# Attention block: the softmax moved to the front of VectorE's period, and two units of the output product's second half begun under the last head

## The chip, the core and the metric

One core of a Trainium2 chip. The metric is device time of one execution in microseconds (us), the median over runs. Engine names in the profile: PE is TensorE's matmul, PEld its weight load, DVE is VectorE, ACT is ScalarE, POOL is GpSimd, SP the engine that issues the DMAs.

## What is computed

Two transformer blocks run one after the other, each of two layers, on 256 tokens (the first one on 272, with 16 tokens put in front) and a model width of 1024, in float32. The first block is FFN, mixer, FFN in each layer. The mixer of its second layer is the one that the change touches, a differential attention with eight heads, cut here to what matters:

```python
q, k, v = jnp.split(h @ w_qkv, 3, axis=-1)      # 8 heads, q and k in two parts of 64, v of 128
q, k = partial_rope(q), partial_rope(k)
...
p = softmax(where(mask, q @ k.T * scale, NEG_INF))
a = p[:, :, 0] - lam * p[:, :, 1]
o = rms_norm(a @ v, subln_g, SUBLN_EPS) * (1.0 - lambda_init)
m = o.reshape(bsz, seq_len, d) @ w_o
h = h + rms_norm(m, g)
```

## The kernel before

**Products.** Activations stand transposed: a chunk is 128 features in the partitions by the tokens in the free dimension, and the width of 1024 is eight chunks. A product with a weight matrix is cut into units. A unit is 128 output features: eight chunks of weights, each 128 by 128. Both operands are split into a high and a low part (`x_hi`, `x_lo`; `w_hi`, `w_lo`), and `product` issues three matmuls for a chunk: high by high, high by low, low by high. So a unit has 24 matmuls. Four units are a quad, and their weights have four slots in SBUF (`raw`, `w_hi`, `w_lo`).

**The path of a unit's weights.** SP loads `raw` of a slot as soon as VectorE has split the slot's previous content (semaphore `w_lo_ready`). ScalarE writes `w_hi` (`split_hi`, line 581) when `raw` has landed and TensorE has finished the slot's previous unit (`unit_done`). VectorE then writes `w_lo` = `raw` - `w_hi` (`split_lo`, line 1046). TensorE waits for `w_lo_ready`. Whole units are split at once, 1024 columns. The stages of the kernel take the slots in turn. Here they are `ain` (the projection to q, k and v, 24 units), `aout` (the output product `w_o`, 8 units in two quads), and then `gu3` (the next FFN).

**The attention.** Every engine has its own list of work, written out by hand in a loop over periods `p`. In period `p` TensorE computes the three units of head `p` (q, k, v) and, between them, the later steps of the heads `p-1` and `p-2`:

```python
for p in range(2, HEADS):
    ain_unit(3 * p)
    swapped(p - 1)
    ain_unit(3 * p + 1)
    attn_t(p - 2)
    ain_unit(3 * p + 2)
    head_sum(p - 2)
    scores(p - 1)
    square_sum(p - 2)
```

`swapped` is a helper product for the rope (lines 1960, 1962). `scores` computes the two score matrices into banks 4 and 6 of PSUM and transposes v (lines 1970 to 1980). `attn_t` transposes the finished probabilities (lines 1987 to 1991); it waits for VectorE's last softmax instruction, `aB` on line 1364. `head_sum` multiplies them with v (lines 1997 to 1999), after ScalarE's copies on lines 808 to 810. `square_sum` sums the squares for the head's norm (line 2003).

ScalarE's part of a head: it takes q and k out of PSUM (lines 799, 804), computes the exponentials (`exps`, four instructions and four reads of the accumulator, line 832), copies the transposed probabilities (`attn_t`), squares the head's output (`out_square`, line 814), computes its norm (lines 603, 605), and a period later writes the high part of the output (`upper_out`, line 838). Between these stand the splits of weights.

VectorE's period is `att_split(u)` (the `w_lo` of one unit), `lower_out(p-3)` (line 1376, the low part of a head's output), `softmax(p-2)` (six instructions, lines 1356 to 1364, that begin when the exponentials of head `p-2` are there), `rope(p-1)` (six instructions, lines 1328 to 1336), `att_split(u+1)`, `value(p)`, `att_split(u+2)`, `maxima(p-1)`, `full_out(p-2)` (line 1371). Each engine does its list strictly in order.

**The output product.** Its first quad needs the heads as its chunks: chunk `k` is head `k`'s output. TensorE takes those chunks in `aout_part` calls as they become ready, mixed with the last heads' steps: before the last head's `attn_t` it computes chunks 0 to 6 of the units 0 to 3, and chunk 7 when the last head is finished. The second quad (`aout_last`) begins after that. Its weights are split in `out1` of ScalarE and `evac_out1` of VectorE: for output `o`, ScalarE waits for the unit, squares it (line 735), takes it out of PSUM with a gain (line 736), and then splits the next unit for the slot. GpSimd adds the squares up (`add0` to `add6`, line 1693). TensorE puts the sum of the seven into the norm's bank (`res_most`, line 1861) before chunk 5 of the last unit, and the eighth square after it (`res_last`, line 1866). From this ScalarE computes the norm (lines 603, 605), VectorE adds it to `h` (lines 1092, 1098), and the next stage's first quad begins (lines 1801 to 1809). `out1_bank` names the PSUM bank of each unit; the norm's sum is always in bank 4.

`vec.phase`, `act.phase` and `pe.phase` at line 344 and after only declare the order in which each engine counts up its semaphore.

## Time and profile before

| | |
|---|---|
| median of 3 runs | 1411.38 us (1411.13 to 1411.57) |
| the profiled execution's own time | 1414.27 us |
| its span in the profile | 1412.5 us |
| mean granted clock of TensorE | 0.982 |
| TensorE busy | 1341.3 us, 95% |
| VectorE busy | 920.4 us, 65% |
| ScalarE busy | 807.2 us, 57% |
| read from HBM | 237.76 MB, 169 GB/s |

The span is the part of the execution that the profile shows, from the first instruction to the last. Busy time of the matmuls is modelled (they overlap), so how far apart two of them start says more than how long each is. "Idle before" in a row, written [1.03 <-DVE arena L1364], is the time for which the engine stood still before that instruction, and what released it. The granted clock is 1.00 at 2.4 GHz and 0.50 at 1.2 GHz; a stretch that has both shows a value between. The attention with its output product lies from about 755 to 902 us of the span.

### The profile page before, as it was taken

How to read it: one execution, taken by the hardware profiler on the slowest of the kernel's cores; microseconds unless marked ns; L12 is line 12 of the kernel's file. 1: busy time of each engine (PE TensorE's matmuls, PEld its weight loads, DVE VectorE, ACT ScalarE, POOL GpSimd, SP SyncE). 2: the span in 40 equal slices, each digit the busy share in tenths (PEclk: the TensorE clock that was granted, in tenths of full speed). 3: DMA queues.
4: the chain of work that ended last, by engine and by line, in shares of the span. 5: the costliest groups of instructions: out<-in, count | busy, mean ns of one | idle time of the engine just before them, and what ended most of it. 6: DMA issues, size and time to landing. Idle time of an engine off the chain costs nothing.

```text
span 1412.5 us, 27540 instructions
## 1 busy us (share of the span) xinstructions
PE 1341.3 (95%) x10214; PEld 1292.3 (91%) x10214; DVE 920.4 (65%) x1522; ACT 807.2 (57%) x1567; POOL 82.1 (6%) x81
## 2 busy tenths in 40 slices
PE   6999999998999999999998998899999899989997
PEld 6999999998999999999998886899999899977786
DVE  6777537856777537777437665677764575666774
ACT  6666534447666536666535553776664444457662
POOL 2000001012000001000001000400000000010000
PEclk9999999999999999999999999999999899999999
DMA  5767653663666653767643331466665153444440
GB/s 199 250 228 239 219 192 107 188 189 114 229 223 245 218 163 98 235 229 251 209 125 120 105 105 46 134 224 223 227 250 166 56 179 120 137 129 148 124 121 31
DMA packets 63313, 239.98 MB, mean 170 GB/s; under 512 B 7024, under 2 KB 8448, under 8 KB 63104
## 3 DMA queue, kind: packets, MB, share of 16 engines
q1 hardware_dynamic: 63168, 238.84, 51.4%
q8 instruction: 56, 0.92, 0.3%
q14 instruction: 25, 0.20, 0.0%
q0 software_dynamic: 64, 0.02, 0.0%
HBM read 237.76 MB, written 1.05 MB: 169 GB/s over the span
## 4 chain that ended last, share of the span: by engine, by line
PE 73%; DVE 12%; ACT 9%; issue 4%; DMA 1%; DVEq 0%; ACTq 0%; SPq 0%
PE bank L1736 19%; PE bank L1738 19%; PE bank L1737 19%; DVE w_lo L1046 5%; ACT w_hi L581 3%; PE bank L1743 3%; ACT ada_raw L657 2%; PE bank L1808 1%; PE bank L1801 1%; PE bank L1809 1%; PE bank L1744 1%; DMA ada_raw<-ada_w 1%; PE bank L2103 1%; DVE ada_raw L1134 1%; ACT ln_t L603 1%
## 5 line engine op out<-in xcount | busy, mean ns | idle before, releaser
L1046 DVE TENSOR_TENSOR w_lo<-raw,w_hi 128x1024 fp32r<-128x1024 f32 (+1 forms) x376 | 493.5, 1316 | 338.8 <-ACT w_hi L581 338.5
L1736 PE MATMUL bank<-x_hl,w_hi 128*128 128x272 f32 (+1 forms) x1776 | 516.3, 291 | 14.6 <-DVE w_lo L1046 14.4
L1738 PE MATMUL bank<-x_hl,w_lo 128*128 128x272 f32 (+1 forms) x1776 | 510.9, 288 | 0.0
L1737 PE MATMUL bank<-x_hl,w_hi 128*128 128x272 f32 (+1 forms) x1776 | 509.1, 287 | 0.0
L581 ACT ACTIVATE w_hi<-raw 128x1024 fp32r<-128x1024 f32 (+1 forms) x376 | 413.8, 1106 | 130.4 <-PE bank L1738 110.8
L1736 PEld LDWEIGHTS bank<-x_hl,w_hi 128*128 128x128 f32 x1776 | 335.6, 189 | 17.7 <-ACT arena L617 8.6
L1737 PEld LDWEIGHTS bank<-x_hl,w_hi 128*128 128x128 f32 x1776 | 338.2, 190 | 0.6
L1738 PEld LDWEIGHTS bank<-x_hl,w_lo 128*128 128x128 f32 x1776 | 335.1, 189 | 0.0
L1736 PE MATMUL bank<-a_hi,w_hi 128*128 128x272 f32 (+1 forms) x960 | 278.8, 290 | 14.5 <-DVE w_lo L1046 3.9
L1738 PE MATMUL bank<-a_hi,w_lo 128*128 128x272 f32 (+1 forms) x960 | 275.3, 287 | 0.0
L1737 PE MATMUL bank<-a_lo,w_hi 128*128 128x272 f32 (+1 forms) x960 | 274.7, 286 | 0.0
L1736 PEld LDWEIGHTS bank<-a_hi,w_hi 128*128 128x128 f32 x960 | 182.5, 190 | 18.1 <-DVE w_lo L1046 7.6
L1737 PEld LDWEIGHTS bank<-a_lo,w_hi 128*128 128x128 f32 x960 | 182.9, 191 | 0.3
L1738 PEld LDWEIGHTS bank<-a_hi,w_lo 128*128 128x128 f32 x960 | 182.3, 190 | 0.0
L657 ACT ACTIVATE ada_raw<-ada_raw,cond 128x128 f32<-128x128 f32 x384 | 117.6, 389 | 0.9 <-DMA ada_raw<-ada_w 0.7
L673 ACT ACTIVATE a_hi<-arena 128x272 f32 (+3 forms) x88 | 37.7, 429 | 125.5 <-DVE arena L1152 125.1
L1743 PE MATMUL bank<-x_hl,w_hi 128*128 128x512 f32 x256 | 93.5, 405 | 4.4 <-DVE x_hl L1084 2.8
L1744 PE MATMUL bank<-x_hl,w_lo 128*128 128x256 f32 x256 | 72.2, 282 | 0.0
L1743 PEld LDWEIGHTS bank<-x_hl,w_hi 128*128 128x128 f32 x256 | 48.7, 190 | 16.2 <-issue 5.0
L1680 POOL TENSOR_TENSOR sq_sum<-sq_sum,sq 128x272 f32<-128x272 f32 (+1 forms) x28 | 21.4, 765 | 701.8 <-ACT sq L706 701.8
L706 ACT ACTIVATE sq<-bank 128x272 f32<-128x272 f32 (+1 forms) x32 | 12.6, 395 | 85.9 <-PE bank L1738 85.9
L1808 PE MATMUL bank<-x_hl,w_hi 128*128 128x272 f32 (+1 forms) x144 | 43.9, 326 | 10.6 <-ACT x_hl L613 8.3
(273 smaller groups left out, 1427.7 us busy)
## 6 DMA issues: line engine op xcount, KB each, us to landing
raw<-w SPq DMA_DIRECT2D x312, 512.0 KB, 4.5
raw<-w SPq DMA_DIRECT2D x64, 704.0 KB, 4.8
ada_raw<-ada_w SPq DMA_DIRECT2D x48, 512.0 KB, 3.6
h<-x_in SPq DMA_DIRECT2D x1, 1088.0 KB, 5.1
work<-bands SPq DMA_DIRECT2D x1, 544.0 KB, 7.0
cst<-consts SPq DMA_DIRECT2D x1, 528.0 KB, 4.6
out<-h SPq DMA_DIRECT2D x1, 512.0 KB, 3.0
out<-h SPq DMA_DIRECT2D x4, 128.0 KB, 2.3
```

The source lines that it names most:

```text
L581: sc.activation(w_hi[:, s, 0:n], raw[:, s, 0:n], ACT.Copy).then_inc(w_hi_ready, 1)
L603: sc.activation(ln_t[:, 0:n], src, ACT.Ln, bias=eps[:, :], scale=scale).then_inc(act.step(phase, "ln"), 1)
L657: last = sc.activation(ada_raw[:, c, :], ada_raw[:, c, :], ACT.Copy, scale=cond[:, c:c + 1])
L673: sc.activation(a_hi[:, bass.ds(2 * i + p, 1), 0:n].rearrange("p a t -> p (a t)"), u_t[:, p, 0:n], ACT.Copy).then_inc(act.step(phase, f"hi ...
L1046: ve.tensor_tensor(w_lo[:, s, 0:n], raw[:, s, 0:n], w_hi[:, s, 0:n].bitcast(F32), ALU.subtract).then_inc(w_lo_ready, 1)
L1680: gp.tensor_tensor(sq_sum[:, 0:n], sq_sum[:, 0:n], sq[:, p, 0:n], ALU.add).then_inc(pool.step(phase, f"add{p}"), 1)
L1736: te.matmul(dst, w_hi[:, s, a:a + P], rhs_hi, start=first, stop=False)
L1737: te.matmul(dst, w_hi[:, s, a:a + P], rhs_lo, start=False, stop=False)
L1738: return te.matmul(dst, w_lo[:, s, a:a + P], rhs_hi, start=False, stop=last)
L1743: te.matmul(dst.rearrange("p (a t) -> p a t", a=2), w_hi[:, s, a:a + P], both, start=first, stop=False)
L1744: return te.matmul(dst[:, 0:SEQ], w_lo[:, s, a:a + P], both[:, 0, :], start=False, stop=last)
L1808: te.matmul(dsts[s][:, 0:n], w_hi[:, s, k * P:(k + 1) * P], x_hi[:, k, 0:n], start=k == 0, stop=False)
```

## The change

In every period VectorE does `softmax(p-2)` first, ahead of `att_split(u)` and `lower_out(p-3)`; before, it came after both.

Of the output product's second quad, chunks 0 to 5 of the units 0, 1 and 2 are computed ahead of the quad's own place: units 0 and 1 around the last head's `square_sum`, ahead of chunk 7 of the first quad, and unit 2 behind unit 1 of the second quad. For that the weights of these three units are split in two pieces. The piece for chunks 0 to 5 (768 columns) is split in period 9 by `early_hi` and `early_lo`, once TensorE has done chunk 5 of the slot's unit of the first quad; the piece for chunks 6 and 7 (256 columns, from `6 * P`) at the old place. In TensorE's list chunk 5 of the units 0 and 1 now comes before unit 3, and chunk 6 of the four units comes behind the last head's transposes instead of ahead of them. The units of the second quad are in other banks (4, 6, 3, 7 for 3, 6, 7, 0), so the wait for the free bank is now `f0` of the second quad, ahead of `res_most`.

```diff
--- before.py
+++ after.py
@@ -344,10 +344,12 @@
 
         vec.phase("att", ["ib", "cb", "cr", "sr"])
         for p in PERIODS:
+            if head(p - 2):
+                vec.phase(f"soft{p - 2}", ["r", "l", "bA", "aA", "bB", "aB"])
             if head(p - 3):
                 vec.phase(f"lo{p - 3}", ["lo"])
-            if head(p - 2):
-                vec.phase(f"soft{p - 2}", ["r", "l", "bA", "aA", "bB", "aB"])
+            if p == HEADS + 1:
+                vec.phase("early", ["lo0", "lo1", "lo2"])
             if head(p - 1):
                 vec.phase(f"rope{p - 1}", ["qc", "kc", "qx", "kx", "qs", "ks"])
             if head(p):
@@ -363,10 +365,14 @@
                 act.phase("preas", ["ln", "r"])
             if head(p - 3):
                 act.phase(f"hi{p - 3}", ["hi"])
+            if p == HEADS + 1:
+                act.phase("early", ["hi0", "hi1"])
             if head(p) and p:
                 act.phase(f"k{p}", ["k"])
             if head(p - 2):
                 act.phase(f"at{p - 2}", ["atm", "at1", "at2"])
+                if p == HEADS + 1:
+                    act.phase("early2", ["hi2"])
                 act.phase(f"osq{p - 2}", ["osq"])
             if head(p - 1):
                 act.phase(f"vn{p - 1}", ["vn", "vm"])
@@ -386,6 +392,8 @@
                 pe.phase(f"s{p - 1}", ["s0", "s1", "vt"])
             if head(p - 2):
                 pe.phase(f"oss{p - 2}", ["oss"])
+            if p == HEADS:
+                pe.phase("early", ["u0", "u1", "u2"])
         declare_out1("aout", "resa")
         declare_enter("pre3")
         declare_ffn(3)
@@ -497,7 +505,9 @@
 
             if stage == "eout":
                 return bank[((6, 7, 0, 1), (2, 3, 5, 6))[i][s]]
-            if stage in ("aout", "oout"):
+            if stage == "aout":
+                return bank[((0, 1, 2, 5), (4, 6, 3, 7))[i][s]]
+            if stage == "oout":
                 return bank[((0, 1, 2, 5), (3, 6, 7, 0))[i][s]]
             return bank[s]
 
@@ -571,14 +581,14 @@
 
         @block.scalar
         def _(sc):
-            def split_hi(stage, i, s):
+            def split_hi(stage, i, s, a=0):
 
                 n = W11 if wide(stage) else W8
                 q = FIRST_QUAD[stage] + i
                 sc.wait_ge(raw_in[s], 16 * q + 16)
                 if not (isinstance(i, int) and q == 0):
                     sc.wait_ge(unit_done, SLOTS * q - SLOTS + s + 1)
-                sc.activation(w_hi[:, s, 0:n], raw[:, s, 0:n], ACT.Copy).then_inc(w_hi_ready, 1)
+                sc.activation(w_hi[:, s, a:n], raw[:, s, a:n], ACT.Copy).then_inc(w_hi_ready, 1)
 
             def split_next(stage, i, s):
 
@@ -734,7 +744,9 @@
                             sc.wait_ge(pool.sem, pool.at(stage, f"add{o - 2}"))
                         sc.activation(sq[:, o % 2, 0:n], out1_bank(stage, i, s)[:, 0:n], ACT.Square).then_inc(act.step(stage, f"sq{s}"), 1)
                         sc.activation(f[:, o, 0:n], out1_bank(stage, i, s)[:, 0:n], ACT.Copy, scale=gain(res, o)).then_inc(act.step(stage, f"f{s}"), 1)
-                        if o < 7:
+                        if stage == "aout" and o < 3:
+                            split_hi(stage, 1, s, 6 * P)
+                        elif o < 7:
                             split_next(stage, i, s)
                 res_norm(res)
 
@@ -837,6 +849,12 @@
                 sc.wait_ge(vec.sem, vec.at(f"full{h}", "full"))
                 sc.activation(a_hi[:, h, META:T], head_out, ACT.Copy).then_inc(act.step(f"hi{h}", "hi"), 1)
 
+            def early_hi(phase, s):
+
+                sc.wait_ge(raw_in[s], 16 * (FIRST_QUAD["aout"] + 1) + 16)
+                sc.wait_ge(pe.sem, pe.at("early", f"u{s}"))
+                sc.activation(w_hi[:, s, 0:6 * P], raw[:, s, 0:6 * P], ACT.Copy).then_inc(act.step(phase, f"hi{s}"), 1)
+
             for p in PERIODS:
                 u = 3 * p
                 if head(p) and p:
@@ -846,11 +864,16 @@
                     token_norm("prea", bank[4])
                 if head(p - 3):
                     upper_out(p - 3)
+                if p == HEADS + 1:
+                    early_hi("early", 0)
+                    early_hi("early", 1)
                 if head(p) and p:
                     raw_k(p)
                     att_split(u + 1)
                 if head(p - 2):
                     attn_t(p - 2)
+                if p == HEADS + 1:
+                    early_hi("early2", 2)
                 if head(p):
                     att_split(u + 2)
                 if head(p - 2):
@@ -1038,12 +1061,12 @@
 
         @block.vector
         def _(ve):
-            def split_lo(stage, i, s):
+            def split_lo(stage, i, s, a=0):
 
                 n = W11 if wide(stage) else W8
                 q = FIRST_QUAD[stage] + i
                 ve.wait_ge(w_hi_ready, SLOTS * q + s + 1)
-                ve.tensor_tensor(w_lo[:, s, 0:n], raw[:, s, 0:n], w_hi[:, s, 0:n].bitcast(F32), ALU.subtract
+                ve.tensor_tensor(w_lo[:, s, a:n], raw[:, s, a:n], w_hi[:, s, a:n].bitcast(F32), ALU.subtract
                                  ).then_inc(w_lo_ready, 1)
 
             def split_next(stage, i, s):
@@ -1214,7 +1237,10 @@
 
             def evac_out1(stage):
                 for o in range(7):
-                    split_next(stage, o // SLOTS, o % SLOTS)
+                    if stage == "aout" and o < 3:
+                        split_lo(stage, 1, o, 6 * P)
+                    else:
+                        split_next(stage, o // SLOTS, o % SLOTS)
 
 
             ve.wait_ge(params_in_, 16)
@@ -1376,14 +1402,25 @@
                 ve.tensor_tensor(a_lo[:, h, META:T], head_out, a_hi[:, h, META:T].bitcast(F32), ALU.subtract
                                  ).then_inc(vec.step(f"lo{h}", "lo"), 1)
 
+            EARLY = 6 * P
+
+            def early_lo(s):
+
+                ve.wait_ge(act.sem, act.at("early2" if s == 2 else "early", f"hi{s}"))
+                ve.tensor_tensor(w_lo[:, s, 0:EARLY], raw[:, s, 0:EARLY], w_hi[:, s, 0:EARLY].bitcast(F32), ALU.subtract
+                                 ).then_inc(vec.step("early", f"lo{s}"), 1)
+
             for p in PERIODS:
                 u = 3 * p
+                if head(p - 2):
+                    softmax(p - 2)
                 if head(p):
                     att_split(u)
                 if head(p - 3):
                     lower_out(p - 3)
-                if head(p - 2):
-                    softmax(p - 2)
+                if p == HEADS + 1:
+                    for s in range(3):
+                        early_lo(s)
                 if head(p - 1):
                     rope(p - 1)
                 if head(p):
@@ -2002,7 +2039,14 @@
                 te.wait_ge(act.sem, act.at(f"osq{h}", "osq"))
                 te.matmul(bank[7][:, 0:SEQ], ones[:, :], sq[:, 0, 0:SEQ], start=True, stop=True).then_inc(pe.step(f"oss{h}", "oss"), 1)
 
-            def aout_part(units, heads):
+            def early_part(s, heads):
+
+                te.wait_ge(vec.sem, vec.at("early", f"lo{s}"))
+                te.wait_ge(act.sem, act.at(f"e{HEADS - 1}", "eB1"))
+                for k in heads:
+                    product(out1_bank("aout", 1, s)[:, 0:SEQ], s, k, a_hi[:, k, META:T], a_lo[:, k, META:T], k == 0, False)
+
+            def aout_part(units, heads, step=None):
 
                 for s in units:
                     te.wait_ge(w_lo_ready, SLOTS * FIRST_QUAD["aout"] + s + 1)
@@ -2013,6 +2057,8 @@
                                        k == 0, k == DC - 1)
                         if k == DC - 1:
                             last.then_inc(unit_done, 1)
+                        if step:
+                            last.then_inc(pe.step(step, f"u{s}"), 1)
 
             te.wait_ge(tables_in, 80)
             swapped(0)
@@ -2041,21 +2087,26 @@
             scores(last)
             square_sum(last - 1)
             te.wait_ge(act.sem, act.at(f"vn{last}", "vm"))
+            aout_part((0, 1), range(5, 6), "early")
             aout_part((3,), range(0, 6))
-            aout_part((0, 1, 2), range(5, 6))
+            aout_part((2,), range(5, 6), "early")
+            attn_t(last)
             aout_part((0, 1, 2, 3), range(6, 7))
-            attn_t(last)
             head_sum(last)
+            early_part(0, range(0, 3))
             square_sum(last)
+            early_part(0, range(3, 6))
+            early_part(1, range(0, 6))
             aout_part((0, 1, 2, 3), range(7, 8))
 
             def aout_last():
                 for s in range(SLOTS):
+                    if s == 2:
+                        early_part(2, range(0, 6))
                     te.wait_ge(w_lo_ready, SLOTS * FIRST_QUAD["aout"] + SLOTS + s + 1)
-                    if s == 3:
-                        te.wait_ge(act.sem, act.at("aout", "f0", 0))
-                    for k in range(DC):
+                    for k in range(6 if s < 3 else 0, DC):
                         if s == 3 and k == 5:
+                            te.wait_ge(act.sem, act.at("aout", "f0", 1))
                             res_most("resa", pool.at("aout", "add6"))
                         last = product(out1_bank("aout", 1, s)[:, 0:SEQ], s, k, a_hi[:, k, META:T], a_lo[:, k, META:T],
                                        k == 0, k == DC - 1)
```

## Rows read from the trace of the kernel before

**Rows 1.** The page: busy us (share of the span) xinstructions by engine.
```profile
PE 1341.3 (95%) x10214; PEld 1292.3 (91%) x10214; DVE 920.4 (65%) x1522; ACT 807.2 (57%) x1567; POOL 82.1 (6%) x81
```

**Rows 2.** Waits from 765 to 857 us: engine, tile, line <- releaser: us, times, longest.
```profile
PEld bank L1987 <- DVE arena L1364: 8.1, 6, 1.8
...
PE bank L1987 <- DVE arena L1364: 6.8, 6, 1.6
```

**Rows 3.** Timeline of one period: start us, us, engine, line, operation, tiles.
```profile
784.36 0.21 ACT L832 ACTIVATION_READ_ACCUMULATOR arena<-bank,small 128x1 f32 x1
...
786.37 1.23 DVE L1046 TENSOR_TENSOR w_lo<-raw,w_hi 128x1024 fp32r<-128x1024 f32 x1 [2.94 <-ACT w_hi L581]
...
787.84 0.17 DVE L1356 RECIPROCAL small<-small 128x4 f32<-128x4 f32 x1
...
788.56 0.29 PE L1738 MATMUL bank<-x_hl,w_lo 128*128 128x272 f32 x1
...
789.32 0.50 DVE L1364 SCALAR_TENSOR_TENSOR arena<-arena,small 128x272 f32<-128x272 f32 x1
...
789.88 0.28 PE L1987 MATMUL bank<-cst,arena 128*16 128x128 f32 x1 [1.03 <-DVE arena L1364]
```

**Rows 4.** Timeline: what comes next in that period.
```profile
791.17 0.25 ACT L810 ACTIVATE arena<-bank 128x128 f32<-128x128 f32 x1
...
799.54 0.21 ACT L832 ACTIVATION_READ_ACCUMULATOR arena<-bank,small 128x1 f32 x1
```

**Rows 5.** Timeline of the last head: its softmax, copies and sums.
```profile
869.98 0.39 PE L1736 MATMUL bank<-a_hi,w_hi 128*128 128x256 f32 x1 [0.19 <-ACT vn L820]
...
872.26 0.21 ACT L832 ACTIVATION_READ_ACCUMULATOR arena<-bank,small 128x1 f32 x1
...
873.15 0.17 DVE L1356 RECIPROCAL small<-small 128x4 f32<-128x4 f32 x1
...
875.19 0.28 PE L1987 MATMUL bank<-cst,arena 128*16 128x128 f32 x1 [0.15 <-DVE arena L1364]
...
876.78 0.69 PE L1997 MATMUL bank<-arena,vn 16*128 16x256 f32 x2 [0.88 <-ACT arena L810]
...
878.80 1.12 PE L2003 MATMUL bank<-sq,ones 128*128 128x256 f32 x2 [0.47 <-ACT sq L814]
...
881.94 0.43 DVE L1376 TENSOR_TENSOR a_lo<-arena,a_hi 128x256 fp32r<-128x256 f32 x1 [0.48 <-ACT a_hi L838]
882.51 0.55 PE L1736 MATMUL bank<-a_hi,w_hi 128*128 128x256 f32 x1 [2.59 <-DVE a_lo L1376]
```

**Rows 6.** Timeline of the output product's second half.
```profile
883.52 0.38 ACT L735 ACTIVATE sq<-bank 128x256 f32<-128x256 f32 x1 [1.62 <-PE bank L1738]
...
884.05 0.73 POOL L1693 TENSOR_TENSOR sq_sum<-sq_sum,sq 128x256 f32<-128x256 f32 x1 [127.89 <-ACT sq L735]
884.16 1.06 ACT L581 ACTIVATE w_hi<-raw 128x1024 fp32r<-128x1024 f32 x1
...
886.53 0.39 PE L1736 MATMUL bank<-a_hi,w_hi 128*128 128x256 f32 x1 [1.12 <-DVE w_lo L1046]
...
887.22 1.53 POOL L1693 TENSOR_TENSOR sq_sum<-sq_sum,sq 128x256 f32<-128x256 f32 x1 [0.15 <-ACT sq L735]
...
896.88 0.59 PE L1861 MATMUL bank<-sq_sum,ones 128*128 128x256 f32 x2
...
898.57 0.38 ACT L735 ACTIVATE sq<-bank 128x256 f32<-128x256 f32 x1 [1.56 <-PE bank L1738]
```

**Rows 7.** Stretches: us, then each engine's busy us and count, granted clock, DMA.
```profile
878.00:885.00 7.00, 3.94 (x17) 3.06 (x15) 0.91 (x2) 3.17 (x7) 0.73 (x1) 0.57 0.01 2
888.00:898.00 10.00, 10.00 (x85) 9.95 (x85) 6.84 (x6) 6.95 (x13) 5.49 (x5) 1.00 0.89 306
902.00:905.40 3.40, 2.98 (x14) 2.71 (x15) 3.25 (x7) 1.97 (x6) 0.00 (x0) 0.62 0.03 8
858.00:865.00 7.00, 5.90 (x45) 5.31 (x45) 4.83 (x15) 3.28 (x14) 0.00 (x0) 1.00 0.16 61
```

## The prediction

> **What bounds the kernel now.** I read the page's busy times first: TensorE is busy for 1341.3 of 1412.5 us, the others for at most 65% [rows 1]. So time can only come from TensorE's gaps or from stretches at its lower clock. Next the list of waits over the attention's periods: TensorE waits there for one thing that counts, the last softmax instruction of VectorE, six times, 6.8 us in all by the matmuls and 8.1 us by the weight loads, which start ahead of them; the longest is 1.6 or 1.8 us [rows 2]. The timeline of one period shows why [rows 3]. The exponentials are finished at 784.57. VectorE stands idle until ScalarE has written the next unit's high part, splits that unit (1.23 us from 786.37), does the low part of a head's output, and begins the softmax only at 787.84. It ends at 789.82, and TensorE, whose unit's last matmul started at 788.56, starts the transposes at 789.88.
>
> Last I read the end of the attention in order of time. TensorE stands idle for 0.88 us before the last head's sum and for 2.59 us before chunk 7 [rows 5], and for 1.12 us before the second quad [rows 6]. From 878 to 885 us the granted clock is 0.57, mostly the lower level of 1.2 GHz, after the stretch with these waits [rows 7].
>
> **The periods.** Moving the softmax adds no instruction. It then follows the exponentials at once, 784.6, and its length is 789.82 - 787.84 = 1.98 us, so it ends at 786.6. TensorE arrives at 788.56 + 0.13 = 788.69 (two neighbouring matmuls of 256 columns start 10.00 / 85 = 0.118 us apart [rows 7], those of 272 columns by that 0.125). The wait goes entirely, with 1.9 us to spare. What it costs is 789.88 - 788.69 = 1.19 us in each of five periods and 1.62 + 0.16 = 1.78 in the first (0.16 is the part of the previous matmul that the next one overlaps): 5 x 1.19 + 1.78 = **7.7 us**. The ends are 6.8 and 8.1 us, the two sums of the wait.
>
> What is late next? The `w_lo` that now stands behind the softmax is that of a unit four units ahead in TensorE's list; it comes about 0.3 us later and is wanted a period later, and SP's next load for that slot moves with it. The rope begins when softmax, split and low part are through (1.98 + 1.23 + 0.42 = 3.6 us after 784.6, so 788.2; it was 789.8), so it moves forward by more than TensorE does. ScalarE's copies of the transposed probabilities ended at 791.42 [rows 4], 1.54 us behind the start of the transposes. TensorE's unit behind them takes 3.2 us. With the copies now behind a split of 1.05 us they end at 2.4 us, still inside it. The next exponentials end at 799.75 [rows 4], 9.87 us after the transposes; a period is 799.54 - 784.36 = 15.2 us and the new one 14.0, so the next softmax (1.98) ends 2 us before it is wanted. Nothing takes the wait's place.
>
> **The last head.** All times from here are in the old trace's own; the 7.7 us come off them all. In period 8 and in the last, the low part (0.43 us, of which the next instruction covers some 0.1) goes behind the softmax. At the last head the exponentials end at 872.47 and the softmax began at 873.15 [rows 5]; it can begin 0.64 us earlier. In period 8 the rope then follows 0.64 - 0.35 = 0.3 us earlier, and the scores with it. So TensorE starts the stretch of 869.98 at 869.7. Matmuls are 0.118 us apart.
> - Ahead of the transposes are now 27 matmuls in place of 39: 3.2 us, 872.9. The softmax ends at 872.47 - 0.3 + 0.04 + 1.98 = 874.2. TensorE waits 1.3 us, a new gap.
> - Transposes 0.55 us, then chunk 6 (12 matmuls, 1.4 us): 876.2. ScalarE's copies take 876.73 - 875.19 = 1.54 us from the transposes' start and end at 875.8. The wait of 0.88 us is gone, covered by chunk 6. ScalarE does two early pieces before these copies, from 872.5, each 0.85 us (between 0.42 for 256 columns and 1.06 for 1024): 874.2, before the transposes. They cost nothing.
> - The head's sum occupies TensorE for 878.80 - 0.47 - 876.78 = 1.55 us: 877.75. VectorE has written the low part of head 6 by 874.6 and the first early piece (0.96 us between 0.43 and 1.23) by 875.6. Then 9 matmuls to 878.8 and `square_sum` to 879.2. From the start of `square_sum` to the end of the low part it took 882.37 - 878.80 = 3.57 us [rows 5]; at the full clock its 1.12 us are some 0.6, so 878.8 + 3.05 = 881.85.
> - Meanwhile TensorE has 9 + 18 matmuls, 3.2 us, to 882.4. So chunk 7 starts at 882.4 against 882.51, with 36 early matmuls done. The old gap of 2.59 us is filled with them.
>
> This assumes the clock of 1.00. The old trace has from 858 to 865 us a similar mix, two short waits with transposes among products, and the clock stayed at 1.00 [rows 7]. So I take it, and price a fall below.
>
> **The second quad.** ScalarE's square of the first unit came 1.01 us after the start of chunk 7, at the lower clock; at the full one I take 0.6 (half is the least): 883.0. Square and eviction take 884.16 - 883.52 = 0.64 us [rows 6], the piece of 256 columns 0.42 on ScalarE and 0.43 on VectorE, where 1024 columns took 1.06 and 1.23. So unit 0's second piece is there at 884.5, and TensorE, through with chunk 7 at 883.8, waits 0.7 us. Six matmuls to 885.25; unit 1's piece is there at 885.5; six more, 886.2. Unit 2 has 18 + 6 matmuls without a wait: 889.0. Unit 3's whole split is there at 888.9. Its first 15 matmuls end at 890.75.
>
> Then stands `res_most`, which needs GpSimd's seventh add. Before, it came at 896.88 just as TensorE arrived. Now ScalarE's order holds it back: from about 885.9 it has three whole splits (0.64 + 0.95 us each) before the seventh square, which ends near 891.1. The add takes between 0.73 and 1.53 us, the two rows of it, the longer one beside a split on VectorE [rows 6]. I put `res_most` at **892.5**, a new wait of 1.75 us. The bounds are 890.75 (no wait) and seven adds of 1.53 in a row from 883.45: 894.2. From there to the eighth square the distance is 898.57 - 896.88 = 1.7 us [rows 6]: 894.2. It was 898.57. The tail gives **4.3 us**, between 2.6 and 6.1.
>
> The next stage's first weights are loaded when a second piece is split, 2 us earlier than before (884.5 for 886.5), and are wanted 4.3 us earlier. So 2.3 us of their slack are used up; the eighth square and the norm still stand before that stage. The DMA engines' share of 0.89 from 888 to 898 [rows 7] says that these loads can't come much faster; rival 2 prices it.
>
> **A rule weighed.** From 878 to 885 us the lower clock held for most of 7 us [rows 7]. The Trainium skill, page "TensorE: Matmul & The Clock Gate", section "Terms", puts the penalty at the throttled time times (1 - K/N), half of it here. By that the old kernel would lose 3.4 us there, and the change would give them back besides its waits. The trace doesn't support so much: only 17 matmuls lie in that stretch, and of its 7 us TensorE was busy for 3.94. My sum takes no separate term for it.
>
> **Sum.** 7.7 + 4.3 = 12.0 us. The profiled execution took 1414.27 us (span 1412.5) and would take 1402.3. The median of the runs is 2.9 us below the profiled one, so 1411.4 - 12.0 = **1399.4 us**. By the low ends, 6.8 + 2.6, it is 1402.0; by the high ones, 8.1 + 6.1, it is 1397.2.
>
> **Rivals.**
> 1. *The clock falls under the last head.* The new gap of 1.3 us stands beside transposes and the head's sum, as those from 871 to 878 did before the fall at 878. A stretch of 3.4 us at the lower level (as 902 to 905.4, clock 0.62 [rows 7]) costs dense work half of it, 1.7 us: 1401.1. Against it: 858 to 865. Chance 0.12.
> 2. *The tail gives next to nothing.* The short pieces, three whole splits and seven adds are one chain through three engines; if the adds run at 1.53 us and the first weights of the next stage land late and block ScalarE, `res_most` comes at 895.5 and the tail gives 1.3 us: 1411.4 - 7.7 - 1.3 = 1402.4. Chance 0.14.
> 3. *The order doesn't do what it says in the periods.* If another wait, of TensorE's `head_sum` for the copies or of `scores` for the rope, takes half of the 7.7 us, it is 1411.4 - 3.9 - 4.3 = 1403.2. Slacks of 0.8 and 2 us speak against it. Chance 0.08.
> 4. *Slower, by the clock behind the attention.* Everything after 902 us comes 12 us earlier against the clock's stretches. Each gap there (first quads of the stages, norms) could then be followed by a lower clock where it wasn't. A stretch costs 1.7 us, so from eight additional ones the gain is gone: 1399.4 + 8 x 1.7 = 1413.0. Nothing in the trace shows so many gaps that are near to a fall. Chance 0.03.
>
> My forecast has 0.63. The range holds one such stretch more or fewer behind the attention and the rivals 1 to 3: 1396.4 to 1404.4. About 0.2% (2.8 us) is what a measurement of this kernel can tell from no change. All cases but the last lie beyond it; with some doubt about them: faster 0.95, same 0.02, slower 0.03.
>
> **What would show it.** In the new trace the waits of line 1987 for 1364 are gone from six periods, and a period is 14.0 us for 15.2; if not, the first term is wrong. One wait of about 1.3 us stays at the last head. 36 matmuls stand between the last head's sum and chunk 7, and no wait for its low part. The second quad begins after a wait of 0.7 us, and `res_most` waits for about 1.75 us; without this wait the tail gives 6 us. A granted clock under 1.00 between the last transposes and `res_most` would be rival 1. A span reduced by less than 9 us would make the whole wrong.

## The result, and the profile after

The changed kernel takes 1400.1 us (median of 6 runs, 1399.22 to 1401.02), the kernel before 1411.47 us beside it (6 runs). The ratio is 0.9914, with a 95% interval of 0.9902 to 0.9926: 11.4 us less, against 12.0 us predicted and 1399.4 us forecast. In two later series one execution each took 4125 us (of the changed kernel) and 7365 us (of the kernel before); medians and differences below are of the others.

Its profiled execution took 1399.22 us. The page's busy times answer to [rows 1]; TensorE's share is the same, of a shorter span:

```profile
PE 1334.0 (95%) x10214; PEld 1288.2 (92%) x10214; DVE 920.1 (66%) x1525; ACT 806.8 (58%) x1570; POOL 81.0 (6%) x81
```

The lines have new numbers: 1364 is now 1390, 1376 is 1402, 1736 to 1738 are 1773 to 1775, 1987 is 2024, 1997 is 2034, 2003 is 2040, 581 is 591, 735 is 745, 1046 is 1069, 1861 is 1898. This execution is 0.8 us late before the attention begins (the first quad of the projection starts at 741.50 for 740.70), so differences of times below have 0.8 us taken off.

The list of TensorE's waits from 765 to 857 us answers to [rows 2]. The wait of the transposes for VectorE is not in it. What is left are two short waits of the `scores` and `swapped` steps, and the kernel before has the same two, of 1.4 and 0.3 us:

```profile
PE bank L2007 <- DVE arena L1362: 1.4, 1, 1.4
PE bank L1997 <- ACT vn L832: 0.3, 1, 0.3
```

The timeline of one period answers to [rows 3]. The last read of the accumulator ends at 825.48 and the softmax begins at 825.50. It ends at 827.49, the split follows it, and the transposes start 0.13 us behind the last matmul of the unit:

```profile
825.26 0.22 ACT L844 ACTIVATION_READ_ACCUMULATOR arena<-bank,small 128x1 f32 x1
...
825.50 0.18 DVE L1382 RECIPROCAL small<-small 128x4 f32<-128x4 f32 x1 [1.18 <-ACT arena L844]
...
826.99 0.50 DVE L1390 SCALAR_TENSOR_TENSOR arena<-arena,small 128x272 f32<-128x272 f32 x1
827.41 1.22 DVE L1069 TENSOR_TENSOR w_lo<-raw,w_hi 128x1024 fp32r<-128x1024 f32 x1
...
829.40 0.29 PE L1775 MATMUL bank<-x_hl,w_lo 128*128 128x272 f32 x1
829.53 0.27 PE L2024 MATMUL bank<-cst,arena 128*16 128x128 f32 x1
```

The timeline of the last head answers to [rows 5]. The transposes now have a wait of 1.11 us, the head's sum has none, and the low part is ready (874.91) while TensorE is still in the early matmuls:

```profile
865.31 0.18 DVE L1382 RECIPROCAL small<-small 128x4 f32<-128x4 f32 x1 [1.17 <-ACT arena L844]
865.46 1.58 ACT L856 ACTIVATE w_hi<-raw 128x768 fp32r<-128x768 f32 x2
...
867.36 0.28 PE L2024 MATMUL bank<-cst,arena 128*16 128x128 f32 x1 [1.11 <-DVE arena L1390]
...
868.65 0.25 ACT L822 ACTIVATE arena<-bank 128x128 f32<-128x128 f32 x1
...
869.42 0.48 PE L2034 MATMUL bank<-arena,vn 16*128 16x256 f32 x1
...
871.86 0.60 PE L2040 MATMUL bank<-sq,ones 128*128 128x256 f32 x2
...
874.48 0.43 DVE L1402 TENSOR_TENSOR a_lo<-arena,a_hi 128x256 fp32r<-128x256 f32 x1 [0.48 <-ACT a_hi L850]
```

The timeline of the second quad answers to [rows 6]. Its wait for the small piece is 0.56 us. ScalarE stands 0.71 us for a load before the split at 883.52; the seventh add starts at 884.99 and takes 1.43 us, and TensorE waits 2.43 us for it:

```profile
876.03 0.38 ACT L745 ACTIVATE sq<-bank 128x256 f32<-128x256 f32 x1 [1.58 <-PE bank L1775]
...
876.67 0.42 ACT L591 ACTIVATE w_hi<-raw 128x256 fp32r<-128x256 f32 x1
...
877.63 0.39 PE L1773 MATMUL bank<-a_hi,w_hi 128*128 128x256 f32 x1 [0.56 <-DVE w_lo L1069]
...
883.52 1.06 ACT L591 ACTIVATE w_hi<-raw 128x1024 fp32r<-128x1024 f32 x1 [0.71 <-DMA raw<-w]
...
884.99 1.43 POOL L1730 TENSOR_TENSOR sq_sum<-sq_sum,sq 128x256 f32<-128x256 f32 x1 [0.90 <-ACT sq L745]
...
886.57 0.95 PE L1898 MATMUL bank<-sq_sum,ones 128*128 128x256 f32 x2 [2.43 <-POOL sq_sum L1730]
...
889.48 0.38 ACT L745 ACTIVATE sq<-bank 128x256 f32<-128x256 f32 x1 [3.32 <-PE bank L1775]
```

The stretches show the clock, as [rows 7] did. It holds at 1.00 under the last head, where before it had fallen to 0.57, and falls behind the wait for the sum, just where the last nine matmuls run:

```profile
871.00:878.00 7.00, 6.43 (x53) 6.18 (x52) 1.37 (x3) 3.66 (x11) 1.23 (x2) 1.00 0.01 2
...
886.80:890.20 3.40, 2.93 (x12) 2.48 (x12) 0.70 (x1) 0.72 (x2) 0.00 (x0) 0.50 1.01 384
```

### The profile page after: what moved, and what is told of

Read it like the earlier page. It is cut to its first block, busy times and chain, and to the rows that moved or that the text cites. A ratio compares the mean times of both kernels' runs of the same rounds, so it can differ in the third digit from the quotient of the medians.

```text
span 1397.4 us, 27554 instructions
## 1 busy us (share of the span) xinstructions
PE 1334.0 (95%) x10214; PEld 1288.2 (92%) x10214; DVE 920.1 (66%) x1525; ACT 806.8 (58%) x1570; POOL 81.0 (6%) x81
## 4 chain that ended last, share of the span: by engine, by line
PE 75%; DVE 10%; ACT 8%; issue 4%; DMA 2%; DVEq 0%; ACTq 0%; POOL 0%; SPq 0%; POOLq 0%
PE bank L1773 20%; PE bank L1775 20%; PE bank L1774 19%; DVE w_lo L1069 4%; PE bank L1780 3%; ACT w_hi L591 2%; ACT ada_raw L667 2%; PE bank L1845 2%; PE bank L1846 1%; PE bank L1838 1%; PE bank L1781 1%; PE bank L2154 1%; DVE ada_raw L1157 1%; DMA ada_raw<-ada_w 1%; DMA raw<-w 1%
## 5 line engine op out<-in xcount | busy, mean ns | idle before, releaser
L1069 DVE TENSOR_TENSOR w_lo<-raw,w_hi 128x1024 fp32r<-128x1024 f32 (+2 forms) x376 | 489.8, 1306 | 321.1 <-ACT w_hi L591 320.6
L591 ACT ACTIVATE w_hi<-raw 128x1024 fp32r<-128x1024 f32 (+2 forms) x376 | 411.9, 1101 | 125.7 <-PE bank L1775 107.1
```

The costliest lines, as they stand in the source:

```text
L591: sc.activation(w_hi[:, s, a:n], raw[:, s, a:n], ACT.Copy).then_inc(w_hi_ready, 1)
L1069: ve.tensor_tensor(w_lo[:, s, a:n], raw[:, s, a:n], w_hi[:, s, a:n].bitcast(F32), ALU.subtract).then_inc(w_lo_ready, 1)
```

## Experiments

For each kernel I read one length from its trace besides its time: from the first matmul of the projection's first quad to the first matmul of the next stage's first quad. It contains the whole attention and output product and nothing else. It is called the attention stretch below. Before it is 902.26 - 740.70 = 161.56 us, after 893.31 - 741.50 = 151.81 us. It is read from one execution of each series. Three traces of the changed kernel differ in it by 0.8 us, two of the kernel with the late sum and late split by 0.3 us, so smaller differences say little.

| kernel | median us | ratio to before (95%) | attention stretch, us |
|---|---|---|---|
| changed | 1400.1 | 0.9914 (0.9902 to 0.9926) | 151.81 |
| changed, second series | 1401.89 | 0.9933 (0.9912 to 0.9954) | 152.56 |
| changed, third series | 1401.08 | 0.9920 (0.9898 to 0.9942) | 151.76 |
| order alone | 1404.76 | 0.9940 (0.9921 to 0.9959) | 154.82 |
| early units alone | 1409.25 | 0.9974 (0.9959 to 0.9989) | 158.91 |
| sum late | 1399.13 | 0.9889 (0.9865 to 0.9913) | 148.88 |
| sum late, split late | 1397.41 | 0.9882 (0.9858 to 0.9905) | 148.47 |
| the same again | 1397.8 | 0.9902 (0.9883 to 0.9922) | 148.16 |
| early products late | 1401.93 | 0.9932 (0.9912 to 0.9952) | 152.65 |
| order, chunk 6 behind | 1403.83 | 0.9948 (0.9927 to 0.9969) | 154.88 |
| the norm's wait filled | 1397.38 | 0.9899 (0.9878 to 0.9920) | 147.82 |
| early products late, sum late | 1401.89 | 0.9928 (0.9909 to 0.9947) | 152.80 |

### The two parts by themselves

Order alone, on the kernel before (with the declared order of the semaphore):

```diff
             for p in PERIODS:
                 u = 3 * p
+                if head(p - 2):
+                    softmax(p - 2)
                 if head(p):
                     att_split(u)
                 if head(p - 3):
                     lower_out(p - 3)
-                if head(p - 2):
-                    softmax(p - 2)
```

> The kernel before with VectorE's new order alone (softmax first in each period); the output product is as before. My theory: the six waits of the transposes go, 7.7 us, and some 0.4 us more at the last two heads, since the old list of TensorE has 39 matmuls ahead of the last transposes: 8.1 us, ratio to before 0.9943; a period is 13.9 us. Rival: the order gives half of that because another wait takes its place, ratio 0.997. Second rival: order and early units depend on one another, and alone the order gives nothing at the last head (7.7 us).

Early units alone is the changed kernel with the same lines put back.

> The changed kernel with VectorE's old order (split and low part ahead of the softmax); early units and two pieces stay. My theory: the periods are 15.1 us again, and the tail alone gives 2.2 us (the eighth square) to 3.4 us (the start of the seven squares' sum), ratio 0.9980. With the order alone at 8.1 the two parts should add up to about 11.4 us, the whole change. Rival: the tail is worth nothing by itself, ratio 1.000, since the clock falls and the adds take it back.

The ratios are 0.9940 and 0.9974, and their product is 0.9914, that of the whole change. In the attention stretch they are 6.7 and 2.7 us, together 9.4 of 9.75 us. So the two parts add up as far as intervals of 0.2% on each ratio can tell, and about seven tenths of the gain is the order.

From the projection's first quad to the sixth transposes the order alone saves 7.8 us (101.86 for 109.64 us), as worked out. But it then loses 1.0 us at the last head, where I had expected 0.4 us more. The timeline shows a wait that I had not seen, ahead of the last transposes:

```profile
869.04 0.36 PE L1736 MATMUL bank<-a_hi,w_hi 128*128 128x256 f32 x1 [1.53 <-DVE a_lo L1376]
...
872.13 0.69 PE L1997 MATMUL bank<-arena,vn 16*128 16x256 f32 x2 [0.88 <-ACT arena L810]
```

Chunk 6 needs head 6's low part, which now comes after the softmax, and in the old list the last transposes stand behind chunk 6. That is what moving chunk 6 behind the transposes avoids. I tried this by itself, on the kernel with the order alone:

```diff
-            aout_part((0, 1, 2, 3), range(6, 7))
             attn_t(last)
+            aout_part((0, 1, 2, 3), range(6, 7))
             head_sum(last)
```

> The kernel with VectorE's order alone, and chunk 6 of the output product moved behind the last head's transposes, as the change has it. My theory: the order alone lost 1 us at the last head, because chunk 6 stood ahead of the transposes and its low part now comes after the softmax (a wait of 1.5 us); behind the transposes chunk 6 also covers the wait of 0.9 us for ScalarE's copies. So about 1.3 us less than the order alone, ratio 0.9930 for 0.9940. Rival: the transposes are bound by the softmax in both, and only 0.3 us or less comes.

The transposes do come 1.9 us earlier after the projection's start (125.77 for 127.68 us), and the wait for the copies is gone. Nothing is left of it at the end: stretch 154.88 for 154.82 us. The clock took it. From about the old wait for the last low part on, it is at its lower level for 10.2 us here and for 6.8 us with the order alone:

```profile
872.20:882.40 10.20, 7.28 (x32) 7.02 (x33) 5.76 (x6) 7.09 (x14) 5.27 (x4) 0.50 0.29 76
```

```profile
874.20:881.00 6.80, 4.03 (x14) 3.05 (x14) 1.25 (x3) 3.37 (x8) 0.73 (x1) 0.50 0.01 2
```

The first row is of the kernel with chunk 6 behind, the second of the order alone. The 1.9 us are still there when the second quad starts, 137.16 us after the projection's start for 139.08. From there to the eighth square's sum it then takes 14.46 us for 12.48. Of the 14.46 us 4.4 are at the lower level, and half of that is 2.2 us; with the order alone the clock is up again before the second quad. The rows of the two starts and the two sums, first with chunk 6 behind, then of the order alone:

```profile
878.02 0.58 PE L1736 MATMUL bank<-a_hi,w_hi 128*128 128x256 f32 x1 [1.12 <-DVE w_lo L1046]
...
892.48 0.70 PE L1866 MATMUL bank<-sq,ones 128*128 128x256 f32 x2 [0.47 <-ACT sq L735]
```

```profile
881.94 0.39 PE L1736 MATMUL bank<-a_hi,w_hi 128*128 128x256 f32 x1 [1.12 <-DVE w_lo L1046]
...
894.42 0.70 PE L1866 MATMUL bank<-sq,ones 128*128 128x256 f32 x2 [0.47 <-ACT sq L735]
```

Theory and rival both asked only what releases the transposes; the lower clock was in neither.

### The sum of the seven squares

The wait of 2.43 us stands in the middle of the last unit because the sum was issued before its chunk 5. I moved it behind the unit:

```diff
                     for k in range(6 if s < 3 else 0, DC):
-                        if s == 3 and k == 5:
-                            te.wait_ge(act.sem, act.at("aout", "f0", 1))
-                            res_most("resa", pool.at("aout", "add6"))
                         last = product(...)
                     last.then_inc(unit_done, 1)
+                te.wait_ge(act.sem, act.at("aout", "f0", 1))
+                res_most("resa", pool.at("aout", "add6"))
                 res_last("resa", act.at("aout", "sq3", 1))
```

> The changed kernel, with the wait for GpSimd's seventh add and the sum of the seven squares moved from chunk 5 of the last unit to behind its last matmul. My theory: TensorE's wait of 2.4 us before that sum goes, the last nine matmuls run at once and at the full clock, and the eighth square comes when ScalarE is through with its split, 2.5 to 3 us earlier: 1397.3 us, ratio 0.990. Rival one: ScalarE's order and GpSimd's adds are the bound whatever TensorE does; the sum then stands in the way itself and the gain is under 1 us. Rival two: the lower clock comes anyway behind this place and takes 1.7 us back.

Then in addition ScalarE's split of the next stage's third unit was put behind the eighth square:

```diff
                         if stage == "aout" and o < 3:
                             split_hi(stage, 1, s, 6 * P)
+                        elif stage == "aout" and o == 6:
+                            pass
+                        elif stage == "aout" and o == 7:
+                            split_next(stage, i, 2)
                         elif o < 7:
                             split_next(stage, i, s)
```

> As the kernel with the late sum, and in addition ScalarE does the split of the next stage's third unit behind the eighth square instead of ahead of it. My theory: the eighth square no longer waits for a split of 1.06 us, and the seventh add is alone with no split on VectorE beside it (0.73 in place of 1.43 us); 0.7 to 1 us less than the kernel with the late sum, ratio 0.9893. Rival: the next stage's first quad then waits for its third unit's low part (split 1.06 + 1.23 us later), and the time is the same or up to 1 us more.

The late sum gives 2.9 us in the stretch, as my theory had it: the wait and the slow matmuls go. In its trace the sum now waits for the eighth square, and that square for ScalarE's split:

```profile
886.44 1.06 ACT L591 ACTIVATE w_hi<-raw 128x1024 fp32r<-128x1024 f32 x1
887.39 0.38 ACT L745 ACTIVATE sq<-bank 128x256 f32<-128x256 f32 x1
...
887.91 0.67 PE L1898 MATMUL bank<-sq_sum,ones 128*128 128x256 f32 x2 [1.63 <-ACT sq L745]
```

So rival one was partly right: ScalarE's order is the next bound, but not at under 1 us. The late split adds 0.4 us in the stretch (expected 0.7 to 1), inside the uncertainty of the times. One of its two reasons failed: the seventh add still takes 1.42 us (884.82 to 886.24), since another split stands on VectorE beside it, from 884.43. The kernel with both was timed again beside the changed one:

> The kernel with the late sum and the late split once more, now on one chip with the changed kernel. Expected 3 to 4 us (0.25%) less than the changed kernel; rival: its lead in the first series came from the chip, and it is within 1 us.

> The changed kernel unaltered, as the reference for the two others of this call. Expected ratio to before 0.991 to 0.9935.

It takes 1397.8 for 1401.08 us, 3.3 us less on the same chip. This version beats both kernels.

### Do the early matmuls pay?

In the changed kernel 36 of them stand under the last head. I moved them to the head of their own units and left the pieces as they were:

```diff
             head_sum(last)
-            early_part(0, range(0, 3))
             square_sum(last)
-            early_part(0, range(3, 6))
-            early_part(1, range(0, 6))
...
-                    if s == 2:
-                        early_part(2, range(0, 6))
+                    if s < 3:
+                        early_part(s, range(0, 6))
```

> The changed kernel, its early products of units 0 and 1 (36 matmuls) moved from under the last head to the head of their own units; the weights are still split in two pieces and as early. My theory: the last head's square sum comes 1.1 us earlier, chunk 7 waits about 2.4 us for the head's low part, but then the second quad runs without a wait: the 18 matmuls at the head of each unit cover the small piece (0.6 us) and the wait for the seven squares' sum (2.4 us) is gone. So the fill under the last head was given back at that sum: time within 1 us of the changed kernel, 1399 to 1401. Rival (the fill is what pays): 36 matmuls of 0.118 us come back on the path, 2.5 to 4 us slower, 1403 to 1404. In both the clock can fall behind the wait of 2.4 us, for another 1 to 1.7 us.

> The changed kernel unaltered, beside the three others of this call on one chip. Expected: ratio 0.991 to 0.992, as before, and the stretch from the first quad of the attention's projection to the first quad of the next stage 9.8 us shorter than in the kernel before, since that stretch was the same in structure. My theory for what is left over: how long the clock stands at its lower level behind the attention differs from one execution to the next, and 1 us of it costs about 0.45 us; the time of each run should follow its mean granted clock. Rival: the part behind the attention is faster by itself, then it is so at the same clock too.

1401.93 and 1401.89 us on the same chip, stretches 152.65 and 152.56. The other two traces of the changed kernel have 151.81 and 151.76, so the two are equal to within 1 us. (The repeat itself missed what I expected of it: its ratio is 0.9933 and its stretch 9.0 us shorter than before, for 0.991 to 0.992 and 9.8 us.) The trace shows the exchange. Chunk 7 waits for the low part again. The second quad then takes TensorE long enough for the adds to be done, and the sum of the seven squares doesn't wait:

```profile
873.96 0.55 PE L1773 MATMUL bank<-a_hi,w_hi 128*128 128x256 f32 x1 [2.59 <-DVE a_lo L1402]
...
888.03 0.59 PE L1898 MATMUL bank<-sq_sum,ones 128*128 128x256 f32 x2
```

The clock is at 0.50 for 6.8 us from 872.3 us on, inside this wait, so the exchange isn't one to one: the fill keeps the clock up under the last head and loses 2.43 to 2.80 us at the sum and 3.4 us at the lower clock behind it. If that reading is right, the fill must pay as soon as the sum is out of the way. That was tried too, the same move on the kernel with the late sum and late split:

> The kernel with the late sum and the late split, its early products moved from under the last head to the head of their own units, as in the run where this made no difference to the changed kernel. My theory: there the fill was given back at the sum of the seven squares; with the sum out of the way it is not, so here the 36 matmuls are on the path and it is 3 to 4 us slower than the kernel with the late sum and late split (eighth square about 149 us after the first quad of the projection, for 145.3). Rival: the 36 matmuls pay nothing in any arrangement, since ScalarE's order of squares and splits sets the end; then both are equal.

1401.89 against 1397.8 us on one chip, 4.1 us slower; the stretch is 4.6 us longer (152.80 for 148.16). So the early products are worth 4 us with the late sum, and nothing, to within 1 us, with the old one. Part of the 4 us is the clock: without the fill it is at 0.50 for 6.8 us from 874.6 us on, inside the wait for the low part, and with it at 1.00 in that place. The runs don't divide the 4 us between waiting and clock.

### The lower clock

Behind the norm the clock fell in each trace (in [rows 7] from 902 us). In the kernel with the late sum and the late split I filled TensorE's wait there with matmuls that nobody reads:

```diff
                 res_last("resa", act.at("aout", "sq3", 1))
+                te.wait_ge(act.sem, act.at("aout", "f0", 0))
+                for n in range(18):
+                    te.matmul(bank[0][:, 0:SEQ], a_hi[:, 0, META:META + P], a_hi[:, 1, META:T], start=True, stop=True)
```

> The kernel with the late sum and the late split, and 18 matmuls of 256 columns whose result nobody reads, behind the eighth square's sum, where TensorE waits 2.6 us for the norm. My theory: the lower clock that follows this wait in every trace (from 889.6 us, 3.4 us long) does not come, and the first quad runs its first chunks at the full clock; since these also wait for ScalarE and VectorE the gain is 0.8 us, at most 1.7. Rival: fp32r products with one bank in a row are not what keeps the clock, it falls all the same and the time is unchanged or 0.3 us longer.

The clock stayed at 1.00 over the place, the first quad's beginning, where the same kernel without the fill has 0.58. First the row with the fill, then that without:

```profile
891.30:894.70 3.40, 2.67 (x18) 2.29 (x19) 3.40 (x8) 1.97 (x6) 0.00 (x0) 1.00 0.55 211
```

```profile
890.10:893.50 3.40, 3.40 (x18) 3.40 (x19) 3.40 (x8) 1.97 (x6) 0.00 (x0) 0.58 0.39 140
```

And it gave next to nothing: from this first quad to that of the stage after the FFN it is 211.53 with and 211.49 us without. The second trace of the kernel without it has 212.13 us: there the quad's fourth unit starts 10.34 us behind its first matmul, for 10.07 us in the first trace and 10.05 us with the fill. So at this place the fill is worth 0.3 us at most. With the clock up, TensorE waits for ScalarE's high parts instead (1.2 us in three waits, where none of them stood behind the first). VectorE is busy for the whole of both rows, so it is most likely the bound there. This holds for a short fall alone: with the early products late the lower clock lasted 6.8 us at this place (from 892.8 us), and the fourth unit started after 11.44 us. My gain of 0.8 us was wrong, and the rival's "falls all the same" too.

Elsewhere the clock costs. The kernel before ran 21 times on one chip, from 1410.14 to 1419.98 us, with mean granted clocks of 0.977 to 0.984. If time at the lower level is 2 x (1 - clock) x time, its times go with it at 0.43 us for each us (correlation 0.94). In six runs of the changed kernel in the second series the correlation is 0.97, in the six of the first only 0.49. The slope isn't a constant either: in the smaller series (5 to 12 runs) it lies between 0.09 and 0.60. What lies behind the attention, from the next stage's first quad to the end, is 510.2 us in the profiled execution before and 504.1 in that of the changed kernel. In the eleven other traces it is 504.2 to 508.1 with the same code. The clock is at its lower level for 30.7 us of it in the trace before and for 17.1 us in that of the changed kernel. So of the 15.1 us between the two spans the attention stretch is 9.75 us, and the rest goes with the clock outside of it. The kernel before has only one trace, so whether that rest is chance or comes from the change isn't shown.

## Why the prediction was right, step by step

**The periods** came out as worked out. The first transposes are 1.73 us earlier (1.78 predicted), the sixth 7.69 us (7.7), and a period is 13.92 us (14.0). The slacks that I worked out held: no new wait appears in this stretch.

**The last head.** Predicted for the transposes 874.2 - 7.7, with the 0.8 us that is 867.3; they start at 867.36. Their new wait is 1.11 us for 1.3. The first unit's square: 876.1 predicted, 876.03 measured. The second quad's start: 877.6 predicted, 877.63 measured. The clock stayed up here, as 858 to 865 us in the old trace let expect [rows 7], so rival 1 didn't happen at its place.

**The sum of the seven squares** is the term that was sized too small. I put it at 892.5, which is 885.6 in the new trace; it came at 886.57. ScalarE's order behind it was right, but a load held it back by 0.71 us, the wait that I had only in rival 2, so the seventh square ended at 884.85 for 884.2. From there to the sum it took 1.7 us (the add 1.43 of them) for the 1.4 us that the 892.5 had held. And the distance from the sum to the eighth square, 1.7 us in the old trace, is 2.9 us, since the clock fell behind the wait: the nine last matmuls ran at 0.50. By the eighth square, the tail and the periods gave 898.57 - 889.48 + 0.8 = 9.9 us in place of 12.0. The tail's share is 2.2 us, half of the 4.3 us and below my low end of 2.6. The loss to the clock is the one of rival 1, but at a place for which I had priced nothing.

**The whole** was still 11.4 us, and here luck has a part: with the 9.75 us of the attention stretch alone, the median would have been 1401.7 us. The two later series have both kernels on one chip. There the medians are 9.4 and 10.0 us apart, which is what the stretches say (9.0 and 9.8 us). The mean granted clocks are 0.9834 before and 0.9843 after in the one, 0.9836 and 0.9848 in the other. That is 3.0 and 3.6 us less at the lower level, and the attention stretch alone has 3.4 us less of it (6.8 us under the old last head, 3.4 us behind the new sum). In the first series the changed kernel's mean clock is higher, 0.9857; the clocks of the six runs beside it weren't recorded, so the 1.4 to 2.0 us above the later series stay unexplained. The hit of 0.7 us is better than the sum behind it.

**What the sum hid.** It gave the tail 4.3 us with the early matmuls as its reason. The runs show that they were worth nothing in this arrangement. The tail's gain in this arrangement comes from the rest of the change. The kernel with the fill moved back (stretch 152.65 us) differs from the one with the order and chunk 6 behind (154.88 us) by the two pieces, the order of chunk 5 and the banks: together 2.2 us, not taken apart. The fill's 4 us went into the wait for the sum and the slow matmuls behind it.

**The rule weighed.** The estimate of the Trainium skill, page "TensorE: Matmul & The Clock Gate", section "Terms" (half of the throttled time, 3.4 us for the old tail), was left out of the sum. Over the 21 executions before, the measured 0.43 us per us is close to its half. So are the 4.4 us at the lower level in the second quad (chunk 6 behind), where TensorE took 2.0 us longer. At one place it is far off: 3.4 us at the lower clock cost 0.3 us at most in the first quad, where VectorE was busy all the time. In these runs the estimate fits where TensorE itself is the bound.

## What to carry to other kernels

When a fill removes a wait on the critical engine, look for the next instruction in its list that needs a chain of the other engines, and ask where it would arrive: here the sum in the middle of the last unit took it back to within 1 us, and moving that one instruction behind the unit made it pay. In an engine's list, the step that another engine waits for goes first in the period, but then check who needs the step that went behind it. Compare small changes by a stretch between two fixed points of the trace besides the total, since total times of one kernel here vary by up to 10 us with the granted clock.

## Not expected of the hardware

- GpSimd's add of 128x256 float32 takes 0.73 us alone and 1.43 to 1.53 us when VectorE subtracts two SBUF tensors of 1024 columns at the same time. With the small pieces (0.46 us on VectorE), each of which overlaps an add by less than 0.2 us, four adds in a row kept 0.73 us.
- Two series gave the same kernel's ratio as 0.9914 and 0.9933; the 21 runs of the kernel before spread by 0.7% on one chip, and there the granted clock goes with most of it (correlation 0.94).
- With 18 unused matmuls in the norm's wait of 2.6 us the clock didn't fall behind it, and 0.3 us at most came of it.
